# A decoder step in float32 on one core: a new order of projections, key products and softmax steps ahead of the experts, extra matmuls in the router, and the slot table behind the first expert

## The reference

```
h = rmsnorm(x);  [u | q | k | v | forget-logits | gate-logits] = h @ w_in       # 1024 -> 512,512,512,512,8,2048
pool = windows of 2,4,8,16 rows over u, less u, times w_pool                     # 4 groups
att  = softmax(q k^T / 8 + c_q - c_k) v      # c = running sum of log-sigmoid forgets, 8 heads of 64
x += (sig(g0) * (pool @ w_up_pool) + sig(g1) * (att @ w_up_att)) @ w_out
h = rmsnorm(x); top-1 of 4 groups, top-2 of its 8 experts (softmax weights)
x += sum over 32 experts of gate * ((silu(h w1) * (h w3)) @ w2)                  # 1024 -> 512 -> 1024
y = rmsnorm(x)
```

## Time and profile before

| | |
|---|---|
| median of 3 runs | 765.18 us (765.14 to 769.54) |
| the profiled execution, device time | 766.7 us |
| its span, first to last instruction | 764.8 us |
| TensorE busy in the span | 612.2 us (80%), mean granted clock 0.892 |
| VectorE, ScalarE, GpSimd busy | 226.0, 84.5, 47.4 us |
| moved by DMA | 269.13 MB, 352 GB/s over the span |
| DMA in slices of 19.1 us from 249 us on | 247, 212, 51, 330, 415 GB/s |
| first part, `forget` to `out` | about 19 to 275 us |
| norm and router | 275 to 298 us |
| experts | 298 to 765 us |

### The profile page before, as it was taken

How to read it: one execution, slowest core, us unless ns; L and a number is a source line. 1 busy time by engine, 2 the same in 40 slices (tenths; PEclk the granted TensorE clock), 3 DMA queues, 4 the chain that set the end, 5 groups by cost and what they waited for, 6 DMA issues and landing times.

```text
span 764.8 us, 13714 instructions
## 1 busy us (share of the span) xinstructions
PE 612.2 (80%) x6150; PEld 370.7 (48%) x6150; DVE 226.0 (30%) x545; ACT 84.5 (11%) x224; POOL 47.4 (6%) x58
## 2 busy tenths in 40 slices
PE   4998799979989988799677768766876778587774
PEld 3777577756566354455344334433443344344332
DVE  3469746791123244322111111111111111111113
ACT  2312123211100201000000000000000000000003
POOL 5014240011100000000000000000000000000000
PEclk9999799998999997899978887988889779878887
DMA  9929969856999651899999999999999999999992
GB/s 325 398 107 386 217 225 259 317 218 257 398 420 420 247 212 51 330 415 422 414 423 424 419 417 423 422 416 420 424 420 417 420 425 417 421 421 419 419 378 94
DMA packets 43514, 269.13 MB, mean 352 GB/s; under 512 B 5076, under 2 KB 5896, under 8 KB 32951
## 3 DMA queue, kind: packets, MB, share of 16 engines
q1 hardware_dynamic: 36736, 230.91, 76.0%
q0 software_dynamic: 3072, 35.19, 11.3%
q10 hardware_dynamic: 3647, 2.14, 1.0%
HBM read 265.99 MB, written 2.46 MB: 351 GB/s over the span
## 4 chain that ended last, share of the span: by engine, by line
PE 40%; DMA 38%; SPq 9%; DVE 7%; issue 3%; ACT 1%; ACTq 1%; DVEq 0%
DMA ring<-w_up 36%; PE bank L1309 9%; SPq L475 8%; PE bank L1387 6%; PE bank L1479 6%; PE bank L1525 4%; PE bank L1540 4%; DVE ring L997 3%; DMA bf<-b_forget 2%; PE bank L1456 2%; SPq L546 2%; PE bank L1292 1%; PE bank L1325 1%; PE bank L1340 1%; PE bank L1490 1%
## 5 line engine op out<-in xcount | busy, mean ns | idle before, releaser
L1309 PE MATMUL bank<-ring,front 128*32 128x256 f32 x2048 | 167.7, 499 | 102.5 <-DMA ring<-w_up 97.8
L1309 PEld LDWEIGHTS bank<-ring,front 128*32 128x32 f32 x2048 | 89.3, 142 | 173.2 <-issue 150.0
L1180 DVE COPY front<-bank 128x256 f32<-128x256 f32 x32 | 13.6, 424 | 244.3 <-PE bank L1309 244.3
L1325 PE MATMUL bank<-ring,front 128*32 128x256 f32 x1024 | 62.3, 384 | 0.7 <-DVE front L1185 0.7
L1479 PE MATMUL bank<-hT,ring 128*128 128x264 f32 x256 | 62.1, 399 | 0.0
L1387 PE MATMUL bank<-hT,ring 128*128 128x264 f32 x256 | 61.1, 400 | 0.0
L1292 PE MATMUL bank<-front 128*32 128x256 f32 (+1 forms) x768 | 54.9, 401 | 0.8 <-DVE front L1096 0.8
L1387 PEld LDWEIGHTS bank<-hT,ring 128*128 128x128 f32 x256 | 50.1, 198 | 10.4 <-issue 1.5
L1479 PEld LDWEIGHTS bank<-hT,ring 128*128 128x128 f32 x256 | 49.1, 196 | 10.3 <-issue 2.2
L810 ACT ACTIVATE front<-bank 128x128 f32<-128x128 f32 x32 | 8.9, 277 | 389.0 <-PE bank L1317 389.0
L1325 PEld LDWEIGHTS bank<-ring,front 128*32 128x32 f32 x1024 | 33.6, 112 | 23.8 <-issue 1.6
(11 more groups left out here) (292 smaller groups left out, 481.3 us busy)
## 6 DMA issues: line engine op xcount, KB each, us to landing
ring<-w_gate SPq DMA_DIRECT2D x31, 2048.0 KB, 33.8
ring<-w_down SPq DMA_DIRECT2D x31, 2048.0 KB, 34.5
ring<-w_up SPq DMA_DIRECT2D x31, 2048.0 KB, 30.9
ring<-w_in SPq DMA_DIRECT2D x8, 2048.0 KB, 21.6
ring<-w_out SPq DMA_DIRECT2D x2, 2048.0 KB, 15.0
front<-q_scratch SPq DMA_DIRECT2D x8, 256.0 KB, 7.7
ring<-w_up_pool SPq DMA_DIRECT2D x1, 2048.0 KB, 13.4
ring<-w_up_att SPq DMA_DIRECT2D x1, 2048.0 KB
```

Source lines behind the costliest of these rows:

```text
L1309: last = m.matmul(bank[GATEUP][32 * g:32 * g + 32, 0:256], xgT[:, k % 2, k // 2], w[:, k, 256 * (g % 2):256 * (g % 2) + 256], start=k == 0 ...
L1325: last = m.matmul(bank[TDOWN][32 * g:32 * g + 32, 0:256], hE[:, j % 2, j // 2], wd[:, j, 256 * g:256 * g + 256], start=j == 0, stop=j == F ...
```

## The change

- The order of `PLAN`: u is projected first, then q, k and v. The first weight load holds all rows of u's 512 columns, the second and third hold the halves of q and k, the fourth all of v's; before, the loads were halves of u with q, and of k with v. `nat` of a projection stands behind the next `proj`. `keys` are spread: some among k, v, and one or two at each gate; before, they stood in fours, and then one at each of gates 0 to 12 with three more behind. The softmax of scores on VectorE and ScalarE is a step of its own (`smax`), one or more steps behind its matmuls. Gate 15 stands ahead of the values of the samples.
- The step `dfin` is gone: the sums are finished in `dsums`, and each `datt` b does its own division (two linked operations).
- The forget bias has its own semaphore and is loaded ahead of `wf`; `forget` waits for `wf` alone.
- GpSimd's first page gathers wait for the third weight load instead of the first.
- `out` waits for one column of the merge at a time.
- `keep_warm`: 7 additional matmuls of 128x256 or 128x512 in `norm` and `route`, whose results nobody reads.
- `list_slots` goes behind w_down of expert 0, in another bank, and what VectorE does with it goes to the end of experts 0 and 1.

```diff
-        PLAN = [("forget", 0), ("proj", CC * C_Q), ("fsum", 0)] + proj(C_Q)[1:] + [("nat", C_Q), ("pages", 0), ("forgetT", 0)]
...
-        PLAN += [("keys", n) for n in range(29, 32)] + [("m1", 0), ("dmax", 0), ("gate", 13), ("dshift", 0), ("dsums", 0), ("gate", 14)]
+            PLAN += [("gate", n)] + BESIDE.get(n, []) + [("keys", i) for i in range(KEYS_AT[n], KEYS_AT[n + 1])]
+        PLAN += [("m1", 0), ("gate", 13), ("dmax", 0), ("gate", 14), ("dshift", 0), ("gate", 15), ("dsums", 0)]
         for b in range(NS):
-            PLAN += [("dpv", b), ("up", b) if b < NS - 1 else ("gate", 15), ("datt", b)]
-        PLAN += [("up", NS - 1), ("dfin", 0)]
+            PLAN += [("dpv", b), ("up", b), ("datt", b)]
         PLAN += [("merge", n) for n in range(DK)] + [("out", 0), ("norm", 0), ("route", 0)]
 
-
-        halves = {i: ((C_Q, C_U), (C_K, C_V))[i // 2] for i in range(4)}
-        uses = {("w", i): (("proj", CC * halves[i][0]), ("proj", CC * halves[i][1] + CC - 1)) for i in range(4)}
+        WHO = ((C_U, C_U), (C_Q, C_K), (C_Q, C_K), (C_V, C_V))
+        uses = {("w", i): (("proj", CC * WHO[i][0]), ("proj", CC * WHO[i][1] + CC - 1)) for i in range(4)}
...
+            elif step == "dsums":
+                assign(SUM, "den")
...
-                if kind == "w":
-                    ks = slice(DK // 2 * (a % 2), DK // 2 * (a % 2) + DK // 2)
+                if kind == "w" and a in (1, 2):
+                    ks = slice(DK // 2 * (a - 1), DK // 2 * a)
                     sp.dma_start(dst.rearrange("p (k n) -> p k n", k=DK // 2),
-                                 w_in[:, a // 2 * D:a // 2 * D + D].rearrange("(p k) n -> p k n", p=P)[:, ks]).then_inc(done, 16)
-                elif kind == "g":
-                    sp.dma_start(dst.rearrange("p (k n) -> p k n", k=DK),
-                                 w_in[:, W_GATE + a * DC:W_GATE + (a + 1) * DC].rearrange("(p k) n -> p k n", p=P)).then_inc(done, 16)
+                                 w_in[:, C_Q * DC:C_Q * DC + D].rearrange("(p k) n -> p k n", p=P)[:, ks]).then_inc(done, 16)
+                elif kind in "wg":
...
-            pool.wait_ge(s_slot[where["w", 0]], 16)
+            pool.wait_ge(s_slot[where["w", 2]], 16)
...
+            for r in (0, 64):
+                act.dma_start(bf[r:r + HEADS], t["b_forget"].rearrange("o n -> n o")).then_inc(in_bf, 16)
             act.dma_start(wf[:, :, 0:HEADS], w_in[:, W_FORGET:W_FORGET + HEADS].rearrange("(p k) n -> p k n", p=P)).then_inc(in_wf, 16)
-            for r in (0, 64):
-                act.dma_start(bf[r:r + HEADS], t["b_forget"].rearrange("o n -> n o")).then_inc(in_wf, 16)
...
-                elif step == "scores":
+                elif step == "smax":
...
-                    elif step == "datt":
-                        v.tensor_copy(attT[:, :, SEQ + a], full("datt", a)[:, 0:CC]).then_inc(taken[CHAIN], 1)
-                    elif step == "dfin":
-                        link(v.tensor_tensor(dens, full("den")[:, 0:NS * HEADS].rearrange("p (b n) -> p b n", b=NS), pnew, ALU.add))
-                        link(v.reciprocal(dens, dens))
-                        dve.wait_ge(*count_taken("datt", NS - 1))
                         for f in range(2):
                             r = slice(HD * f, HD * f + HD)
-                            pn, dn = (a8.rearrange("p b (c f) -> p f c b", f=2)[r, f] for a8 in (pnew, dens))
-                            link(v.tensor_tensor(prod[r, f], sT[r, C_V], pn, ALU.mult))
-                            link(v.tensor_tensor(prod[r, f], prod[r, f], attT[r, :, SEQ:TOK], ALU.add))
-                            ins = v.tensor_tensor(attT[r, :, SEQ:TOK], prod[r, f], dn, ALU.mult)
-                        ins.then_inc(taken[CHAIN], 1)
-                    elif step == "scores":
+                            ins = v.tensor_tensor(prod[r, 0], sT[r, C_V], pnew.rearrange("p b (c f) -> p f c b", f=2)[r, f], ALU.mult)
+                        link(ins)
+                        link(v.tensor_tensor(dens, full("den")[:, 0:NS * HEADS].rearrange("p (b n) -> p b n", b=NS), pnew, ALU.add))
+                        for f in range(2):
+                            r = slice(HD * f, HD * f + HD)
+                            ins = v.reciprocal(prod[r, 1], dens.rearrange("p b (c f) -> p f c b", f=2)[r, f])
+                        ins.then_inc(taken[SUM], 1)
+                        dve.wait_ge(*count_taken("den"))
+                    elif step == "datt":
+                        link(v.tensor_tensor(prod[:, 0, :, a], full("datt", a)[:, 0:CC], prod[:, 0, :, a], ALU.add))
+                        v.tensor_tensor(attT[:, :, SEQ + a], prod[:, 0, :, a], prod[:, 1, :, a], ALU.mult).then_inc(taken[CHAIN], 1)
+                    elif step == "smax":
...
                 turned(0)
 
+            def slot_table():
...
+            def list_blocks():
...
-                return_map(e % 2, tabs[:, e:e + 1], tabs[:, EXPERTS + e:EXPERTS + e + 1])
+                if e:
+                    return_map(e % 2, tabs[:, e:e + 1], tabs[:, EXPERTS + e:EXPERTS + e + 1])
                 hidden(e)
                 rows(e, e % 2)
                 if e < LAST:
                     turned(e + 1)
+                if e == 0:
+                    slot_table()
+                    dve.wait_ge(l_dve, links[0])
+                    return_map(0, tabs[:, 0:1], tabs[:, EXPERTS:EXPERTS + 1])
+                if e == 1:
+                    list_blocks()
...
+            def keep_warm(b, n):
+
+                m.matmul(bank[b][:, 0:n * P], ident, ident.unsqueeze(1).to_broadcast([P, n, P]), start=True, stop=True, skip_group_check=True)
...
-                    pe.wait_ge(in_wf, 16 * 3)
+                    pe.wait_ge(in_wf, 16)
...
-                elif step == "dfin":
+                elif step == "dsums":
                     out = free("den")
                     pe.wait_ge(s_psm, 1)
-                    m.matmul(out[:, 0:NS * HEADS], ones, sums.rearrange("p b n -> p (b n)"), start=True, stop=True).then_inc(filled[CHAIN], 1)
+                    m.matmul(out[:, 0:NS * HEADS], ones, sums.rearrange("p b n -> p (b n)"), start=True, stop=True).then_inc(filled[SUM], 1)
...
-                        pe.wait_ge(*count_taken("den"))
+                        pe.wait_ge(*count_taken("datt", NS - 1))
...
-                    pe.wait_ge(s_merge, DK)
                     for half in range(2):
                         out = free("opart", half)
                         for k in range(DK):
+                            pe.wait_ge(s_merge, k + 1)
...
                     transposes(range(3, 5))
+                    pe.wait_ge(*count_taken("datt", NS - 1))
+                    keep_warm(CHAIN, 4)
...
                     inject()
+                    keep_warm(PART, 4)
+                    keep_warm(PART, 2)
...
                     gather(0)
+                    keep_warm(PART, 2)
                     turn_tokens(0)
+                    keep_warm(PART, 2)
...
-                else:
-                    list_slots()
-                    pe.wait_ge(*count_taken("tables"))
...
+                if e == 0:
+                    list_slots()
+                    pe.wait_ge(*count_taken("tables"))
...
```

44 lines of the change are left out of this document (25 added, 19 removed).

## The result

| | before | after |
|---|---|---|
| median | 767.17 us of 4 runs (765.14 to 769.54) | 740.88 us of 4 runs (739.83 to 742.7) |
| profiled execution, span | 766.7, 764.8 | 739.83, 737.9 |
| mean granted clock | 0.892 | 0.905 |

The ratio is 0.9659, with a 95% interval of 0.9615 to 0.9702: faster. The span is 26.9 us shorter, where my sum had 20.4; by the medians 26.3 are saved.

A forecast was written before the change was run, and what follows sets the result against it. From 324 us the experts' weight stream was taken as the bound, and TensorE ahead of the stream's start. The terms summed to 20.4 us off the 765.2 median, giving 744.8, with a range of 740.0 to 753.0.

The forecast's parts named there:

- the start: `forget` and first `proj`: no change, first `proj` still at about 21 us; bounds 1 us lost, 3 gained.
- waits of `nat` and others: TensorE's waits before `nat`, `forgetT` and `pv` vanish behind a `proj` or `gate`: 4.0 us off.
- `snew`, wait and clock behind it: TensorE still waits some 5 us for VectorE's key products, half clock stays: no change; bounds 1 gained, 2 lost.
- the race to `dmax`, clock behind it: From `snew` to `dmax`, TensorE arrives 1.4 us before VectorE: 6.4 off; bounds 0 and 7.8.
- loads behind the order: Gate loads, query spreads and K gathers have thin cover in the new order: 1.0 us lost, bounds 0 and 13.
- merge, `dfin`, `out`: Waits and half clock at the merge and the wait before `out` go, less 0.6 for divisions: 5.0 us off.
- router: Faster gathers and `keep_warm` holding the clock for expert 0: 2.5 us off, bounds 0 and 2.6.
- slot table: Moved behind expert 0's w_down, it no longer delays the start of the weight stream: 3.5 us off, bounds 2 and 4.9.
- more at the start and in VectorE's race: Rival: u's load fast, `dmax` without wait, smaller start-up, 3 + 1.4 + 1 = 5 more, 740 us; chance 0.15.
- About 20: Sign after the change: L1322 of expert 0 about 20 us earlier relative to its end at 304.4.
- One sign of being wrong: VectorE waiting on page gathers or queries between 110 and 160 us, or `wr` copied later than 115.
- the other thin place: Last two query spreads stand behind two gate loads in SP's one queue; within the 1.0 us lost for loads.

The follow-up runs named there:

- e9: Changed kernel with the first 2 MB weight load in 4 KB instead of 2 KB rows, leaving out u's own weights; 745.74 us, one run.
- e3: Kernel before the change, with only the bias issued ahead of `wf` and `forget` waiting for `wf` alone; 772.76 us, one run.
- e5: Changed kernel with q's sample rows turned back one `proj` earlier, right behind q's last `proj`; 738.26 us, ratio 0.9613.
- e6: Changed kernel with each softmax right behind its score matmuls, as before the change; 748.03 us.
- e8: Changed kernel with one key product at each of gates 0 to 11 and the last eight in a row behind gate 12; 753.92 us, one run.
- e7: Changed kernel with GpSimd's copies of the router's weights moved behind the gathers of K for samples 5 to 7; 743.02 us, one run.
- e1: Changed kernel without its seven `keep_warm` matmuls; 742.0 us, ratio 0.967.
- e4: Changed kernel with the slot table ahead of w_down of expert 0 again; 744.63 us, ratio 0.9686.
- e12: Changed kernel with `out` waiting for all eight columns of the merge at once, as before the change; 740.36 us, one run.
- e10: The e5 kernel with three more `keep_warm` matmuls in TensorE's wait before `forget`; 737.41 us, ratio 0.9604.

## Why the prediction was right in its range, and which terms were wrong

| term | predicted | measured |
|---|---|---|
| the start | 0 | 3.0 |
| waits of `nat` and others | 4.0 | 2.2 |
| `snew`, wait and clock behind it | 0 | 3.8 |
| the race to `dmax`, clock behind it | 6.4 | 6.9 |
| loads behind the order | -1.0 | 0 |
| merge, `dfin`, `out` | 5.0 | 5.0 |
| router | 2.5 | 2.5 |
| slot table | 3.5 | 3.6 |

The measured column adds up to 27.0 (0.1 is rounding); that of `nat` is what the other terms leave of the 13.8 up to `dmax` (172.30 less 162.21, and a gate of 3.7 more now stands ahead of it). The terms missed by 3.0, 3.8, 1.0, 0.5 and 0.1 on one side and by 1.8 on the other; `snew`'s 3.8 is outside the bounds of its own term (1 gained, 2 lost), and the start's 3.0 at the edge of its (3 gained). That the time still lies in the range, by 0.9, is in part luck. The rival "more at the start and in VectorE's race" forecast 740, and its time came, but only in part for its reasons: its 3 at the start came in full, its 1.4 at `dmax` as 0.5 and its 1 of start-up as 0.1, and 3.8 came at `snew`, which it did not name.

Of the signs that I had named, L1322 of expert 0 ended 23.3 earlier (281.1 for 304.4). "About 20" was a slip there: the sum without the slot table gives 16.9. One sign of being wrong appeared as well, VectorE's wait of 2.0 for a query at 149 us. In the race I wrote 6.6 for the wait for the first scores where its terms give 6.8; it was 4.7.

**The start: the step that failed.** I took the lone gate load of 151 GB/s as the measure for a load of 2 KB rows, so that u's load would end at 20.9. It was there when the first `proj` wanted it, at 17.89, without a wait; the queues together moved 411 to 413 GB/s just before. The effect lay elsewhere, in the upper bound that I had left as such: `forget` could start 3.0 earlier, and with 4 KB rows in the first load it is 5.5 later again (e9). That 3.0 is a net: issuing `wf` behind the bias cost 4.5 beside the old loads (e3). The rule of the Trainium skill that I had weighed (DMA: Bandwidth & Descriptors, section SWDGE vs HWDGE vs iDMA: each DMA engine takes turns between its queues) agrees with the trace in its direction: small packets get by sooner where their neighbours are shorter, with the reservation named at e9. The lesson in the sum: where row and rule were about different quantities (u's own load, and `wf`), I let the one outvote the other.

**`snew`.** Here the mechanism was right (VectorE's start decides; there was a wait and a half-clock `proj`), and the term was mis-sized. The step "from the end of q's `nat` to the first product were 7.6 us" carried over a figure from full queues. Then, q's write was issued at 39.26 and its spread only at 42.99, with 367 GB/s moving from 39 to 41 us; after the change it is 54.75 and 56.24, at 11 GB/s, 5.3 in all. With that 2.3 my sum gives a wait of 2.6; it was 3.0, for 5.4 before. Of the half clock 1.8 remains (the `proj` behind takes 5.5) instead of 3.2, the scores being far enough behind. e5 shows that most of the rest of the wait hung on when VectorE can start.

**The race to `dmax`.** Predicted 1.4 late, measured 0.9, and the gate behind it ran 3.80, at full clock. e6 and e8 show its two supports, each worth more than any other part that was taken back here: the distance of the softmax from its scores (7.2) and the spreading (about 13, one run). These are what the changed kernel would lose without them, not shares of the 26.9.

**Loads.** VectorE waited for no gather of K, but 2.0 for the query spread of key 28, which I had named as the other thin place; it can have cost no more than the 0.9 at `dmax`. That the gathers stand behind the router's wait is no cost; e7 shows that it is a gain of 3.2 by its rows (2.1 by its single time).

**Waits of `nat`.** One `nat` kept 0.7, since two now stand in a row and share ScalarE; `pv` kept 0.7 and `pT` got 0.6. I had struck them all because a `proj` or `gate` stands between; for these three it doesn't, or the chain on VectorE and ScalarE is longer than the gate; which of the two it is, no run tells apart. Two waits of 0.2 ahead of gates are new.

**Merge, router, slot table** came as computed. e1 shows 2.4 for the router by its rows, e4 3.7 for the slot table by the medians. Of the 5.0 at the merge and `out` only the last piece was taken back by itself (e12: 0.9 for 1.3); the rest is read from the rows before and after.

## What to carry to other kernels

In a list that all engines walk through, give each consumer on another engine a distance of one step from its producer before anything else, and spread long work over many steps: taking them back cost 7 and 13 us here. A wait ahead of large matmuls can cost twice, by itself and in the clock behind it: 3.0 at `snew` brought 1.8 more, while 0.9 at `dmax` brought nothing. Matmuls that nobody reads, fitted into the wait, give the second part back (2.4 in e1, 2.1 in e10). A small load that everything waits for depends on the form of the large loads beside it (5.5 in e9), and a transfer's price from one moment holds only where the queues are as full as then (7.6 and 5.3 for q). Issuing a transfer earlier can cost, where it takes the queues from a small one that is needed first (3.2 in e7).
